# Latent attention in a two-layer encoder: probabilities scaled ahead of their turn, values at rest in the second product

## The chip, the core and the metric

The kernel runs on one core of a Trainium2 chip. The time is the device time of one execution in microseconds; before the change it is 1680.26 us, the median of three runs (1680.10 to 1680.61). The core has five engines with their own instruction queues: PE (TensorE, with PEld for its weight loads), DVE (VectorE), ACT (ScalarE), POOL (GpSimd) and SP (SyncE, which here issues the weight transfers). They meet by semaphores alone. TensorE writes its products into PSUM, which has eight banks; ACT and DVE read them out from there.

## What is computed

A trunk of two layers over 256 tokens, width 1024. Each layer normalises, projects once into three token mixers and three gates, merges the mixers, and goes on with a feed-forward part (dense in the first layer, eight experts in the second). The change lies in the third mixer, the latent attention, with eight heads of 64 values:

```python
for i in range(S // Q_BLOCK):                     # two blocks of 128 queries
    q0, k_end = i * Q_BLOCK, (i + 1) * Q_BLOCK
    s = (...q_nope k_nope + q_pe k_pe...) * scale
    s = jnp.where(k_chunk[None, :] <= q_chunk[:, None], s, -1e30)
    pr = jax.nn.softmax(s, axis=-1).astype(v.dtype)
    outs.append(jnp.einsum('bhqk,bkhe->bqhe', pr, v[:, :k_end]))
...
branch = jnp.einsum('bsnc,ncd->bsnd', ys, w_branch[l])   # ys: the three mixers' outputs
merged = jnp.sum(gates * branch, axis=2)
```

The first 128 queries see 128 keys and the second 128 see 256, so a head has 3 x 128 columns of probabilities.

## The kernel before

**The attention loop.** The loop over `i` stands once for each engine (lines 1580, 1150 and 2357), and the engines walk it together. In iteration `i`, PE computes the scores of head `i` (`sM`, lines 1587 and 1588), two units of the gate projection (line 1427; a unit is three fp32r products of 512 columns), then turns the probabilities of head `i - 1` with three transposes (`pT`, line 1595), multiplies the turned probabilities of head `i - 2` with the values (`oM`, lines 1601 to 1603: the probabilities are the weights at rest, 128x128, and 64 columns of values stream), and does two more gate units. DVE masks and scales the scores of head `i` into `sm`, takes the row maxima (lines 2364 to 2373), makes the low part of a gate weight quarter (`g_low`, line 2375, printed as line 2136), and for head `i - 2` takes the reciprocal of the row sum `den` and multiplies it onto the product while reading it out into `y_mla` (lines 2384 and 2387). In iterations 1 and 2 it also scales the retention's output `y_ret` (1024 columns each time). ACT exponentiates in place with the row sums accumulated (lines 1153 and 1155), copies the turned probabilities of head `i - 1` from PSUM to `pT` (line 1158, printed as 987), and at `i == 3` it applies the sigmoid to two gate tiles (lines 1160 and 1161), for which it loads another table and loads the exponential's again afterwards. POOL makes the high parts of the gate weights.

**After the loop** PE turns the inputs of the second mixer (`kT`, 16 transposes, line 1577, copied to `tT` by ACT), multiplies the last head, ends a gate panel with units 46 and 47, and turns the retention's output (`yT0`, line 1626). ACT then has a sigmoid with its table load again (`gate(4)`, `gate(5)`), and the copies of `yT0`, for which the second half of the products at line 1663 waits.

**The turn of the attention's output.** `y_mla` holds tokens in partitions. The branch projection needs channels there, so in the middle of the second mixer, for `t == 0`, PE turns it with eight transposes (`branch_in(2)`, line 1767, printed as 1626) and ACT copies it to `yT[2]` in two pieces (line 1228). They stand between the products of line 1731 and gate units 64 and 65.

**What sets the order.** Everything is written out by hand. `layer_jobs` lists each PSUM tile in the order in which PE makes it, with the engine that frees it; `place_jobs` gives each the bank that has been idle longest, and `bank(job)` makes PE wait until the tile before it in that bank has been freed. `read_out` waits until a tile has been read out. The weights come through a ring of three slots, filled by SP in the order of `panels`.

Of the kernel before, what the change touches and what calls it, by code (L numbers as in the profile page):

```python
# [17 lines left out]
P = 128  # L18
# [124 lines left out]
def layer_jobs(l):  # L143
# [15 lines left out]
    for i in range(NH + 2):  # L159
        out += [(f"sM{i}", V)] * (i < NH) + [(f"pT{i - 1}", A)] * (0 < i <= NH)  # L160
        out += [(f"kT0{hp}", A) for hp in range(4)] * (i > NH)
        out += [(f"oM{i - 2}", V)] * (i > 1)
        out += [(f"gt{2 + i // 8 * 2 + t}", A) for t in range(T if i == 3 or i > NH else 0)]
    out += [("yT00", A), ("yT01", A)]
    for t in range(T):
        out += [(f"kT1{hp}", A) for hp in range(4)] * t
        out += [(f"M{t}{i}", V) for i in PAIRED] + [(f"br0{t}{t}", V)]
        out += [(f"B{t}{u}", A) for u in range(NH // 2)]
        out += [("gt8", A), ("gt9", A), ("br210", V)] if t else [("gt6", A), ("gt7", A)]
        out += [(f"I{t}{g}", A) for g in range(2)]  # L170
        for lv in range(LEVELS):
            out += [(f"T{t}{lv}{g}", V) for g in range(2)]
            for g in range(2):
                out += [(f"X{t}{lv}{g}", V)] * (lv < LEVELS - 1) + [(f"XT{t}{lv}{g}", V)]
        out += [(("br001", "br201")[t], V), (f"Z{t}", A)] + [(f"W{t}{c}", A) for c in range(2)]
        out += [("yT10", A), ("dU20", V), ("dU21", V)] if t else [("yT20", A), ("yT21", A)]
        out += [(f"U{t}", A)]
        if t == 0:
            out += [("S1", V), ("br010", V), ("dU10", V), ("dU11", V), ("br200", V), ("S2", V)]
        else:  # L180
            out += [("S3", V), ("dU30", V), ("dU31", V), ("br211", V)]
        out += [(f"Y{t}{e}", A) for e in range(2)]
# [127 lines left out]
class Signals:  # L310


    def __init__(self, nc):
# [69 lines left out]
        self.prob_ready = new("prob_ready")  # L383
        self.merged_done = new("merged_done")
# [38 lines left out]
def build(nc, x, positions, all_gains, w_in, rwkv_mu, rwkv_w0, rwkv_w2, rwkv_a0, rwkv_a2, rwkv_g2, rwkv_k_k,  # L423
# [5 lines left out]
    def sb(name, shape, dt=F32, where=None):  # L429
# [29 lines left out]
    y_mla = sb("y_mla", [P, T, W], where=hn_at + 4096)  # L459
# [59 lines left out]
    yT = {n: sb(f"yT{n}", [P, 4, SEQ], where=w) for n, w in ((0, scratch + 4096), (2, ec_at - 4096))}  # L519
    yT1_hi = sb("yT1_hi", [P, 4, SEQ], F32R, where=scratch)  # L520
    yT1_lo = sb("yT1_lo", [P, 4, SEQ], F32R, where=hn_at + 4096)
# [4 lines left out]
        (B + 24576, B + 28672, B + 32768, B + 36864, B + 40960, scratch + 8192, B + 53248, ec_at - 4096))]  # L526
# [218 lines left out]
    def _(sp):  # L745
# [21 lines left out]
        for n, (kind, l, j, _) in enumerate(PANELS):  # L767
# [33 lines left out]
            elif kind == "mla":  # L801
                sp.dma_start(slot[:, 0:1536].rearrange("p (c n) -> p c n", c=2), rows(mla_w_qb[l])).then_inc(sem, 16)
                sp.dma_start(slot[:, 1536:2560], mla_w_kvb[l]).then_inc(sem, 16)
            elif kind == "branch":
# [163 lines left out]
    def _(act):  # L968
# [23 lines left out]
        for l in range(DEPTH):  # L992
# [156 lines left out]
            gate(1)  # L1149
            for i in range(NH + 1):  # L1150
                if i < NH:
# [4 lines left out]
                                          bias=smax[:, i, 1:2], accum_out=den[:, i, 1:2]), s.prob_ready)  # L1156
                if i:
                    copy_out(f"pT{i - 1}.{l}", pT[:, (i - 1) % 2, :], 384)
# [39 lines left out]
            for t in range(T):  # L1198
                for hp in range(4):
                    copy_out(f"kT{t}{hp}.{l}", tT[:, hp, :])  # L1200
                if t == 0:
                    gate(4)
                    gate(5)
# [23 lines left out]
                for u in range(0 if t else 2):  # L1227
                    copy_out(f"yT2{u}.{l}", yT[2][:, 2 * u:2 * u + 2, :])
# [138 lines left out]
    def _(pe):  # L1367
# [70 lines left out]
        for l in range(DEPTH):  # L1438
# [141 lines left out]
            for i in range(NH + 2):  # L1580
# [8 lines left out]
                if i < NH:  # L1589
                    gate_units(16 + 4 * i, 18 + 4 * i)  # L1590
                if 0 < i <= NH:
                    pe.wait_ge(s.prob_ready, NH * l + i)
# [23 lines left out]
            def branch_in(n):  # L1616

                if n == 2:
                    read_out(pe, f"oM{NH - 1}.{l}")
                else:  # L1620
                    pe.wait_ge(s.ret_done, l + 1)
                for u in range(2):
                    b = bank(f"yT{n}{u}.{l}")
                    for i in range(2):
                        for t in range(T):
                            ins = TR(b[:, 256 * i + 128 * t:256 * i + 128 * t + 128],
                                     (y_ret, None, y_mla)[n][:, t, 2 * u + i:W:4], ident)
                    done(ins)

            def branch_slot(n):  # L1630

                slot = panel_of("branch", l, n)
                read_out(pe, f"yT{n}1.{l}" if n != 1 else f"yT10.{l}")
# [16 lines left out]
            for t in range(T):  # L1650
                if t == 0:
                    branch_in(0)
# [113 lines left out]
                else:  # L1766
                    branch_in(2)
# [362 lines left out]
    def _(dve):  # L2130
# [56 lines left out]
        for l in range(DEPTH):  # L2187
# [169 lines left out]
            for i in range(NH + 2):  # L2357
# [16 lines left out]
                if i <= NH:  # L2374
                    g_low(6 + i)
# [638 lines left out]
```

## Time and profile before

| | |
|---|---|
| median of three runs | 1680.26 us (1680.10 to 1680.61) |
| span of the profiled execution | 1678.8 us |
| PE busy | 1624.5 us, 97% |
| DVE busy | 642.3 us, 38% |
| ACT busy | 444.0 us, 26% |
| granted TensorE clock, mean | 0.997 |
| attention loop, layer 0 | 146.6 to 180.5 us |
| turn of the attention's output, layer 0 | 219 us |

The span runs from the first to the last instruction of one profiled execution; the page shows no other time of that execution, and the timed runs are 1.5 us longer (1680.26 - 1678.8). Times inside the program are counted from the span's start. A row of a timeline has its start, its duration and the idle time that came before it on its engine, with what ended it. Durations of neighbouring PE rows overlap, because products are pipelined: what one costs is read from start to start. The chain of waits goes by ends, so the same instruction stands there about 0.2 us later.

### The profile page before, as it was taken

What the parts mean: (1) busy time and instruction counts of PE and PEld (TensorE: products, weight loads), DVE (VectorE), ACT (ScalarE), POOL (GpSimd) and SP (SyncE); (2) the same over time, 40 slices, a digit from 0 to 9 for tenths busy, and PEclk for the clock granted to TensorE, in tenths of its full rate; (3) what the DMA queues carried; (4) which work ended last, traced back from release to release, by engine and by line L of the source; (5) the groups of instructions that cost most, each with busy time, mean ns of one, the idle gap of its engine ahead of it and who ended that gap; (6) DMA issues with size and microseconds to landing.
All of it is one profiled execution on the core that took longest, in us unless ns stands there. A gap on an engine that the chain in (4) does not pass through costs nothing.

```text
span 1678.8 us, 34618 instructions
## 1 busy us (share of the span) xinstructions
PE 1624.5 (97%) x15590; PEld 1016.0 (61%) x15590; DVE 642.3 (38%) x1037; ACT 444.0 (26%) x652; POOL 171.7 (10%) x172
## 2 busy tenths in 40 slices
PE   8999999999999999999999999989999799999996
PEld 7878777788888877877754436343362434634433
DVE  6668666655555669657532010000100001000012
ACT  5477423454344566423410000000000000000001
POOL 1264002200000075100400000000000000000010
PEclk9999999999999999999999999999999999999998
DMA  9645213555445743212799999999999999999996
GB/s 347 234 146 201 86 63 118 212 203 186 171 170 201 225 175 110 101 52 101 306 425 429 428 430 428 429 429 429 429 428 427 429 429 429 428 428 420 406 427 256
DMA packets 84250, 494.14 MB, mean 294 GB/s; under 512 B 5528, under 2 KB 14612, under 8 KB 60632
## 3 DMA queue, kind: packets, MB, share of 16 engines
q1 hardware_dynamic: 79360, 480.52, 71.0%
q0 software_dynamic: 2064, 7.67, 1.2%
q10 hardware_dynamic: 2680, 3.74, 0.7%
q8 instruction: 124, 2.03, 0.4%
q14 instruction: 22, 0.18, 0.0%
HBM read 484.78 MB, written 6.16 MB: 292 GB/s over the span
## 4 chain that ended last, share of the span: by engine, by line
PE 81%; DMA 10%; DVE 6%; ACT 2%; issue 1%; SPq 0%; DVEq 0%; ACTq 0%
PE bank L1427 30%; PE bank L2073 26%; PE bank L2092 11%; DMA slot<-moe_units_dram 9%; PE bank L1642 3%; PE bank L1613 2%; PE bank L1419 2%; PE bank L2035 1%; PE bank L2007 1%; DVE ring_lo L2136 1%; DVE tmp L2136 0%; DMA ring<-w_in_dram 0%; PE bank L1997 0%; DVE xterm L2136 0%; DVE xc L2489 0%
## 5 line engine op out<-in xcount | busy, mean ns | idle before, releaser
L2073 PE MATMUL bank<-slot,xg 128*32 128x512 f32 (+1 forms) x5120 | 489.3, 539 | 8.9 <-DMA slot<-moe_units_dram 8.2
L2073 PEld LDWEIGHTS bank<-slot,xg 128*32 128x32 f32 x5120 | 168.5, 110 | 314.4 <-issue 278.7
L2092 PE MATMUL bank<-slot,ehT 128*32 128x256 f32 x4480 | 250.6, 381 | 25.3 <-DMA slot<-moe_units_dram 24.4
L2092 PEld LDWEIGHTS bank<-slot,ehT 128*32 128x32 f32 x4480 | 143.0, 110 | 127.7 <-DMA slot<-moe_units_dram 33.4
L2136 DVE TENSOR_TENSOR ehm<-bank,esg 128x512 f32<-128x512 f32 (+3 forms) x32 | 23.7, 741 | 463.6 <-ACT esg L1329 463.6
L1329 ACT ACTIVATE esg<-bank 128x512 f32<-128x512 f32 (+3 forms) x32 | 20.4, 637 | 491.9 <-PE bank L2073 491.9
L1427 PE MATMUL bank<-i_hi,ix_hi 128*128 128x512 f32 (+2 forms) x288 | 108.4, 376 | 2.0 <-DVE ix_lo L2136 1.0
L1427 PE MATMUL bank<-i_hi,ix_lo 128*128 128x512 f32 (+2 forms) x288 | 107.9, 375 | 0.0
L1427 PE MATMUL bank<-ring_lo,ix_hi 128*128 128x512 f32 (+2 forms) x288 | 107.8, 374 | 0.0
L2136 DVE TENSOR_TENSOR ring_lo<-ring,i_hi 128x2048 fp32r<-128x2048 f32 (+2 forms) x36 | 80.4, 2240 | 61.5 <-ACT i_hi L1007 61.5
L2908 DVE COPY ehT<-bank 128x512 f32<-128x512 f32 (+3 forms) x32 | 23.7, 741 | 208.6 <-PE bank L2035 203.0
L2136 DVE TENSOR_TENSOR ring_lo<-ring,f_hi 128x2048 fp32r<-128x2048 f32 (+1 forms) x36 | 75.5, 2112 | 63.4 <-ACT f_hi L1256 63.4
L1427 PE MATMUL bank<-g_hi,gx_hi 128*128 128x512 f32 x192 | 84.7, 441 | 0.5 <-DVE ring_lo L2136 0.5
L957 POOL TENSOR_TENSOR place_f<-place_f,cst 128x4 f32<-128x4 f32 x1 | 0.2, 194 | 773.2 <-PE bank L2073 773.2
L1427 PE MATMUL bank<-g_hi,gx_lo 128*128 128x512 f32 x192 | 75.3, 392 | 0.0
L1427 PE MATMUL bank<-ring_lo,gx_hi 128*128 128x512 f32 x192 | 75.2, 392 | 0.0
L1427 PE MATMUL bank<-f_hi,fx_hi 128*128 128x512 f32 (+1 forms) x192 | 71.7, 374 | 0.0
L1427 PE MATMUL bank<-f_hi,fx_lo 128*128 128x512 f32 (+1 forms) x192 | 71.3, 372 | 0.0
L1427 PE MATMUL bank<-ring_lo,fx_hi 128*128 128x512 f32 (+1 forms) x192 | 71.3, 371 | 0.0
L1256 ACT ACTIVATE f_hi<-ring 128x2048 fp32r<-128x2048 f32 (+1 forms) x36 | 62.6, 1770 | 32.5 <-DMA ring<-ffn_w_down_dram 18.5
L1007 ACT ACTIVATE i_hi<-ring 128x2048 fp32r<-128x2048 f32 (+2 forms) x36 | 62.8, 1788 | 24.0 <-issue 11.6
L2136 DVE TENSOR_TENSOR ring_lo<-ring,g_hi 128x1024 fp32r<-128x1024 f32 x48 | 61.7, 1288 | 5.8 <-POOL g_hi L932 4.5
(490 smaller groups left out, 2238.4 us busy)
## 6 DMA issues: line engine op xcount, KB each, us to landing
slot<-moe_units_dram SPq DMA_DIRECT2D x166, 2048.0 KB, 29.5
ring<-w_in_dram SPq DMA_DIRECT2D x25, 2048.0 KB, 8.9
ring<-w_branch_dram SPq DMA_DIRECT2D x6, 2048.0 KB, 7.9
ring<-ffn_w_gate_dram SPq DMA_DIRECT2D x5, 2048.0 KB, 7.9
ring<-ffn_w_up_dram SPq DMA_DIRECT2D x5, 2048.0 KB, 7.8
ring<-ffn_w_down_dram SPq DMA_DIRECT2D x5, 2048.0 KB, 7.9
ring<-w_o_dram SPq DMA_DIRECT2D x2, 2048.0 KB, 8.8
ring<-w_o_dram SPq DMA_DIRECT2D x4, 1024.0 KB, 6.2
```

Of the source, the lines that this page charges most:

```text
L1007: own.step(A.activation(i_hi[:, (q + 1) % 4, 0:width], src, ACT.Copy), s.i_hi_ready)
L1256: own.step(A.activation(f_hi[:, q % 4, 0:width], src, ACT.Copy), s.f_hi_ready)
L1329: A.activation(by_group(esg[:, 0:width], r), gate_, ACT.Silu).then_inc(s.silu_ready, 1)
L1419: ins = M(b[:, 0:width], lhs[:, c, t * P:(t + 1) * P], w[:, c, c0:c0 + width], start=c == 0, stop=c == k - 1)
L1427: ins = M(dst, a[:, c, tok], v[:, cols], start=start and n == 0, stop=stop and n == 2, skip_group_check=True)
L1613: ins = M(b[ch, cols], left[ch, :], right[ch, :], start=True, stop=True)
L1642: ins = M(dst[:], yT[n][:, c, t * P:(t + 1) * P], slot[:, D * c + 512 * u:D * c + 512 * u + 512], start=c == 0, stop=c == 3, skip_group_ch ...
L2007: ins = M(psum[:, to:to + SEL], h[:, t, c * P:c * P + P], sel[:, t, :], start=t == 0, stop=t == T - 1)
L2073: ins = M(psum[GROUP * p:GROUP * p + GROUP, to:to + width], xg[:, x, o:o + GROUP], w[:, c, p, :], start=x == 0 and to % 512 == 0, stop=x = ...
L2092: ins = M(psum[GROUP * p:GROUP * p + GROUP, o:o + 256], ehT[:, x, GROUP * i:GROUP * i + GROUP], w[:, c, p, :], start=x == 0 and o % 512 == ...
L2136: return V.tensor_tensor(out_, a, b, op)
L2908: V.tensor_copy(ehT[:, 8 * r:8 * r + n, 0:tokens].rearrange("p c (g k) -> p g c k", k=GROUP), psum[:, TURN:TURN + n * tokens].rearrange("p ...
```

## The change

For each head DVE now waits in the same iteration for the exponentials, takes the reciprocal of `den`, and multiplies it onto the probabilities in `sm` (128 and 256 columns) before PE turns them; PE's transposes wait for this (`scaled_ready`) instead of for the exponential. The second product is made for two heads at once, in the iterations 3, 5 and 7 and after the loop's last turn (`oP0` to `oP3`), with the values as weights at rest (128x64) and the turned probabilities streaming (256 and 128 columns); one head of a pair writes the bank's partitions 0 to 63, the other 64 to 127. The result has its channels in partitions, ACT copies it into `yT[2]`, and `y_mla`, its eight transposes and two copies are gone. The branch weights of the attention are loaded with another order of rows, in pieces of 1024 columns. Three buffers change places.

```diff
     for i in range(NH + 2):
-        out += [(f"sM{i}", V)] * (i < NH) + [(f"pT{i - 1}", A)] * (0 < i <= NH)
+        out += [(f"sM{i}", V)] * (i < NH)
         out += [(f"kT0{hp}", A) for hp in range(4)] * (i > NH)
-        out += [(f"oM{i - 2}", V)] * (i > 1)
+        out += [(f"oP{(i - 3) // 2}", A)] * (i > 2 and i % 2)
+        out += [(f"pT{i - 1}", A)] * (0 < i <= NH)
...
-        out += [("yT10", A), ("dU20", V), ("dU21", V)] if t else [("yT20", A), ("yT21", A)]
+        out += [("yT10", A), ("dU20", V), ("dU21", V)] if t else []
...
+            elif kind == "branch" and j == 2:
+                sp.dma_start(slot.rearrange("p (c n) -> p c n", c=4), w_branch[l, j].rearrange("(c p) n -> p c n", p=P))\
+                    .then_inc(sem, 16)
...
+            def latent_out(k):
+
+                copy_out(f"oP{k}.{l}", yT[2][:, k, :], SEQ)
+
             for i in range(NH + 1):
...
+                if i > 2 and i % 2:
+                    latent_out((i - 3) // 2)
                 if i:
                     copy_out(f"pT{i - 1}.{l}", pT[:, (i - 1) % 2, :], 384)
...
                 if t == 0:
+                    latent_out(3)
                     gate(4)
...
-                for u in range(0 if t else 2):
-                    copy_out(f"yT2{u}.{l}", yT[2][:, 2 * u:2 * u + 2, :])
...
+                if i > 2 and i % 2:
+                    k = (i - 3) // 2
+                    read_out(pe, f"pT{2 * k + 1}.{l}")
+                    b = bank(f"oP{k}.{l}")
+                    for c in range(T):
+                        for e in range(2):
+                            ins = M(b[64 * e:64 * e + 64, P * c:SEQ], mv[:, c, 2 * k + e, :],
+                                    pT[:, e, SEQ * c:SEQ + P * c], start=c == 0, stop=c == 1, skip_group_check=True)
+                    done(ins)
                 if 0 < i <= NH:
-                    pe.wait_ge(s.prob_ready, NH * l + i)
+                    pe.wait_ge(s.scaled_ready, NH * l + i)
...
-                if i > 1:
-                    k = i - 2
-                    read_out(pe, f"pT{k}.{l}")
-                    b = bank(f"oM{k}.{l}")
-                    M(b[:, 0:64], pT[:, k % 2, 0:128], mv[:, 0, k, :], start=True, stop=True)
-                    M(b[:, 64:128], pT[:, k % 2, 128:256], mv[:, 0, k, :], start=True, stop=False)
-                    done(M(b[:, 64:128], pT[:, k % 2, 256:384], mv[:, 1, k, :], start=False, stop=True))
...
                 else:
-                    branch_in(2)
                     gate_units(64, 66)
...
-                if i > 1:
-                    j = i - 2
-                    dve.wait_ge(s.prob_ready, NH * l + j + 1)
-                    step(V.reciprocal(den[:, j, :], den[:, j, :]))
-                    b = product(dve, f"oM{j}.{l}")
+                if i < NH:
+                    dve.wait_ge(s.prob_ready, NH * l + i + 1)
+                    step(V.reciprocal(den[:, i, :], den[:, i, :]))
                     settle()
-                    free(tt(y_mla[:, :, 64 * j:64 * j + 64], b[:, 0:128].rearrange("p (t e) -> p t e", t=T),
-                            wide(den[:, j, :], HD), ALU.mult), f"oM{j}.{l}")
+                    for t, keys in enumerate((slice(0, P), slice(P, 384))):
+                        step(V.tensor_scalar(sm[:, i % 2, keys], sm[:, i % 2, keys], den[:, i, t:t + 1], None, ALU.mult),
+                             s.scaled_ready if t else None)
```

**PE at the end of the attention loop of layer 0.** Before, from the gate products of iteration 7 on (`sm` holds the probabilities, `mv` the values, `kk` and `pr` are inputs of the second mixer):

```order
L1427 MATMUL bank<-g_hi_138,gx_lo 128x512
L1595 MATMUL bank<-cst,sm 128x128 x3
L1601 MATMUL bank<-mv,pT 128x64
L1602 MATMUL bank<-mv,pT 128x64
L1603 MATMUL bank<-mv,pT 128x64
L1595 MATMUL bank<-cst,sm 128x128 x3
L1601 MATMUL bank<-mv,pT 128x64
L1602 MATMUL bank<-mv,pT 128x64
L1603 MATMUL bank<-mv,pT 128x64
L1577 MATMUL bank<-cst,kk 128x128
```

And the same place in the changed kernel:

```order
L1437 MATMUL bank<-g_hi_137,gx_lo 128x512
L1607 MATMUL bank<-pT,mv 64x256 x2
L1607 MATMUL bank<-pT,mv 64x128 x2
L1614 MATMUL bank<-cst,sm 128x128 x6
L1587 MATMUL bank<-cst,kk 128x128
```

The pair product `oP2` now stands ahead of the transposes, the turns of heads 6 and 7 follow each other with nothing between them, and the inputs of the second mixer are turned right behind the last head.

**ACT from the exponential of head 3 to that of head 4.** Before (`sm,den` is the exponential with its row sum, `sig` the sigmoid of the gates):

```order
L1153 ACTIVATE sm,den<-sm,smax 128x128
L1155 ACTIVATE sm,den<-sm,smax 128x256
L987 ACTIVATE pT<-bank 128x384
L1142 ACT_TABLE_LOAD
L1142 ACTIVATE sig_113<-bank,stat 128x512 x2
L1153 ACT_TABLE_LOAD
L1153 ACTIVATE sm,den<-sm,smax 128x128
L1155 ACTIVATE sm,den<-sm,smax 128x256
L987 ACTIVATE pT<-bank 128x384
```

In the changed kernel:

```order
L1162 ACTIVATE sm,den<-sm,smax 128x128
L1164 ACTIVATE sm,den<-sm,smax 128x256
L991 ACTIVATE yT_116<-bank 128x256
L991 ACTIVATE pT<-bank 128x384
L1146 ACT_TABLE_LOAD
L1146 ACTIVATE sig_112<-bank,stat 128x512 x2
L1162 ACT_TABLE_LOAD
L1162 ACTIVATE sm,den<-sm,smax 128x128
L1164 ACTIVATE sm,den<-sm,smax 128x256
L991 ACTIVATE pT<-bank 128x384
```

The copy of the pair product comes in front of the copy of the turned probabilities; the two table loads and the sigmoids stay where they were, ahead of the exponential of head 4.

## Rows read from the trace of the kernel before

**Rows 1.** the page, section 2 (DMA, 40 slices) and section 4 (chain by engine)

```profile
DMA  9645213555445743212799999999999999999996
...
PE 81%; DMA 10%; DVE 6%; ACT 2%; issue 1%; SPq 0%; DVEq 0%; ACTq 0%
```

**Rows 2.** timeline of PE in the attention of layer 0: start us, us, instruction

```profile
152.02 0.49 PE L1595 MATMUL bank<-cst,sm 128*128 128x128 f32 x3
152.26 0.48 PE L1427 MATMUL bank<-g_hi,gx_hi 128*128 128x512 f32 x1
...
169.07 0.49 PE L1595 MATMUL bank<-cst,sm 128*128 128x128 f32 x3
...
169.99 0.48 PE L1427 MATMUL bank<-g_hi,gx_hi 128*128 128x512 f32 x1
...
175.90 0.39 PE L1587 MATMUL bank<-mkT,mqT 96*128 96x128 f32 x2
...
179.37 0.55 PE L1595 MATMUL bank<-cst,sm 128*128 128x128 f32 x3 [0.32 <-ACT sm L1155]
...
180.46 0.28 PE L1577 MATMUL bank<-cst,kk 128*128 128x128 f32 x1
...
182.21 0.33 PE L1601 MATMUL bank<-mv,pT 128*128 128x64 f32 x2
```

**Rows 3.** chain of waits, 219 to 225 us: start us, us, what

```profile
219.31 1.16 PE bank L1626 x8
220.47 1.40 PE bank L1427 x6
221.87 1.08 PE bank L1613 x32
222.95 1.58 PE bank L1427 x6
```

**Rows 4.** chain of waits, 183 us: the sigmoid table load after the attention

```profile
183.18 1.28 ACT L1142
```

**Rows 5.** timeline of ACT, 160 to 167 us and at 219 us

```profile
160.65 0.40 ACT L1153 ACTIVATE sm<-sm,smax 128x128 f32<-128x128 f32 x1 [2.81 <-DVE smax L2373]
...
162.03 1.28 ACT L1142 ACT_TABLE_LOAD   x1
...
165.90 0.40 ACT L1153 ACTIVATE sm<-sm,smax 128x128 f32<-128x128 f32 x1
...
166.80 0.47 ACT L987 ACTIVATE pT<-bank 128x384 f32<-128x384 f32 x1
...
219.09 0.66 ACT L987 ACTIVATE nw<-bank 128x256 f32<-128x256 f32 x2
```

**Rows 6.** timeline of DVE, 150 to 159 us: heads 1 to 3

```profile
150.83 0.29 DVE L2364 SCALAR_TENSOR_TENSOR sm<-bank,cst 128x128 f32<-128x128 f32 x1 [0.73 <-PE bank L1588]
...
154.91 0.29 DVE L2364 SCALAR_TENSOR_TENSOR sm<-bank,cst 128x128 f32<-128x128 f32 x1
...
157.48 1.22 DVE L2136 TENSOR_TENSOR y_ret<-y_ret,raw 128x1024 f32<-128x1024 f32 x1
158.62 0.15 DVE L2384 RECIPROCAL den<-den 128x2 f32<-128x2 f32 x1
158.88 0.29 DVE L2136 TENSOR_TENSOR y_mla<-bank,den 128x128 f32<-128x128 f32 x1
159.09 0.28 DVE L2364 SCALAR_TENSOR_TENSOR sm<-bank,cst 128x128 f32<-128x128 f32 x1
```

**Rows 7.** instructions of line 2291: duration ns min/median/max

```profile
L2291 DVE TENSOR_SCALAR qa<-qa,stat x4: 348/352/353, 109.2 to 621.5; 128x256 f32<-128x256 f32 x4
```

**Rows 8.** timelines of PE at 224 us and of PEld at 870 us

```profile
224.62 0.29 PE L1758 MATMUL bank<-pr 64*64 64x64 f32 x4
224.74 0.33 PE L1757 MATMUL bank<-uu,ab 64*64 64x64 f32 x4
...
870.41 0.16 PEld L2073 LDWEIGHTS bank<-slot,xg 128*32 128x32 f32 x4 [0.27 <-issue]
```

More of the change, by code:

```diff
@@ L383, in __init__ @@
         self.prob_ready = new("prob_ready")
+        self.scaled_ready = new("scaled_ready")
         self.merged_done = new("merged_done")
@@ L458, in build @@
     y_ret = sb("y_ret", [P, T, W], where=hn_at)
-    y_mla = sb("y_mla", [P, T, W], where=hn_at + 4096)
     ring_at = at[0]
@@ L517, in build @@
     assert VEC_AT["lnx"][0] * 4 >= 16384
-    yT = {n: sb(f"yT{n}", [P, 4, SEQ], where=w) for n, w in ((0, scratch + 4096), (2, ec_at - 4096))}
+    yT = {n: sb(f"yT{n}", [P, 4, SEQ], where=w) for n, w in ((0, scratch + 4096), (2, hn_at + 4096))}
     yT1_hi = sb("yT1_hi", [P, 4, SEQ], F32R, where=scratch)
-    yT1_lo = sb("yT1_lo", [P, 4, SEQ], F32R, where=hn_at + 4096)
+    yT1_lo = sb("yT1_lo", [P, 4, SEQ], F32R, where=ec_at - 4096)
     gT_hi = sb("gT_hi", [P, KD, SEQ], F32R, where=B + 16384)
@@ L525, in build @@
     k_hi = [sb(f"k_hi{n}", [P, QUARTER], F32R, where=w) for n, w in enumerate(
-        (B + 24576, B + 28672, B + 32768, B + 36864, B + 40960, scratch + 8192, B + 53248, ec_at - 4096))]
+        (B + 24576, B + 28672, B + 32768, B + 36864, B + 40960, scratch + 8192, B + 53248, hn_at + 4096))]
     k_hi_last = {n: sb(f"k_hi_last{n}", [P, QUARTER], F32R, where=w) for n, w in ((5, B + 45056), (7, B + 49152))}
@@ L1614, in by_chunk, with turn_retention @@
                 return ins
[L1616 to L1621, printed above, removed]
+            def turn_retention():
+                pe.wait_ge(s.ret_done, l + 1)
                 for u in range(2):
-                    b = bank(f"yT{n}{u}.{l}")
+                    b = bank(f"yT0{u}.{l}")
                     for i in range(2):
                         for t in range(T):
-                            ins = TR(b[:, 256 * i + 128 * t:256 * i + 128 * t + 128],
-                                     (y_ret, None, y_mla)[n][:, t, 2 * u + i:W:4], ident)
+                            ins = TR(b[:, 256 * i + 128 * t:256 * i + 128 * t + 128], y_ret[:, t, 2 * u + i:W:4], ident)
                     done(ins)
@@ L1632, in branch_slot @@
                 slot = panel_of("branch", l, n)
-                read_out(pe, f"yT{n}1.{l}" if n != 1 else f"yT10.{l}")
+                read_out(pe, ("yT01", "yT10", "oP3")[n] + f".{l}")
                 return slot
@@ L1651, in _ @@
                 if t == 0:
-                    branch_in(0)
+                    turn_retention()
                 else:
@@ L2355, in _ @@
             g_low(5)
-            for i in range(NH + 2):
+            for i in range(NH + 1):
                 if i < NH:
@@ L2373, in _ @@
                     step(V.tensor_scalar(smax[:, i, :], smax[:, i, :], -1.0, None, ALU.mult), s.masked_ready)
-                if i <= NH:
-                    g_low(6 + i)
+                g_low(6 + i)
                 if i == 1:
```

## The prediction, made before the changed kernel was run

> **What bounds the kernel now.** I read the page first: TensorE is busy in 97% of the span, and the chain of work that ended last runs through PE for 81% of it, through the DMA for 10% [rows 1]. The DMA share stands in the last half, where every slice reads 9. That is the expert stage, behind the second layer: it starts when the second layer ends and is bound by its own weight stream, so a microsecond that a layer gives up comes out at the end unchanged. The attention and the second mixer stand once in each layer, and layer 1 repeats layer 0; each gain below counts twice. The second view was the timeline of PE in the attention. PE stands still there only once, for 0.32 us ahead of the last head's turn [rows 2] (start 179.37): from the exponential of head 7 on, the heads' chain through PE, DVE and ACT decides, not PE's work. Third, the timelines of ACT and DVE over the same heads: both have gaps in a steady iteration (ACT 2.81 us ahead of head 3's exponential) [rows 5, 6], but two stretches have none. DVE runs on without a pause from head 2 to head 3, because the retention's multiplies stand there [rows 6], and ACT has one block from the exponential of head 3 to that of head 4, 165.90 - 160.65 = 5.25 us with two sigmoids between two table loads [rows 5]. Behind the attention the chain goes over ACT: its table load starts at 183.18 [rows 4]. In the second mixer it runs over PE without a gap at the eight transposes [rows 3].
>
> **What goes.** One head's product `oM` costs PE (169.99 - 169.07) - (152.26 - 152.02) = 0.92 - 0.24 = 0.68 us: the first distance, from a turn to the next gate product, has it, the second hasn't [rows 2]. Eight go. The transposes of `y_mla` go too: with them the gate units start 1.16 us later and take 1.40; without them the units follow the 64x64 products directly, as they do further down, where they take 1.58. So 1.16 + 1.40 - 1.58 = 0.98 us per layer [rows 3]. This is the path, and what is late next there is still PE: the 64x64 products follow the gates immediately. ACT's two copies of `yT[2]` lay beside PE and give nothing.
>
> **What comes: the pair product.** Each of two heads needs 256 + 128 = 384 streamed fp32 columns, in its own 64 columns of the array. The trace doesn't have such a product. The nearest row is the 64x64 work of the second mixer: four instructions, two products in each of two quarters of the array, follow the next four after 224.74 - 224.62 = 0.12 us [rows 8]. At 0.115 us for 64 columns in both, 384 columns cost 6 x 0.115 = 0.69 us if the two heads run side by side, and 1.38 if they run one after the other. That column tiles do run side by side with all 128 rows in use, I take from the expert stage: four weight loads of 128x32 every 0.16 + 0.27 = 0.43 us, a group for four tiles [rows 8]. A gate product behind the tiles is 1.58 - 1.40 = 0.18 us late [rows 3], and the 32 small products take 1.08 where 8 x 0.115 = 0.92 is their work, 0.16 to get in [rows 3, 8]. So X, the cost of a pair product, is 0.69 + 0.18 + 0.16 = 1.03 us; I take 1.04. The bounds are 0.69 (the two switches cost nothing, for the halves stand in one column split and keep all rows) and 1.38 + 0.35 = 1.73.
>
> The Trainium skill bears on both parts. "TensorEngine Tiling (Array Packing)", Key Properties, says that a change of the tiling mode drains the engine; the 0.18 us of [rows 3] agree. "TensorE: Matmul & The Clock Gate", Part 3 (The mechanism), says that products start and end strictly in program order. As the fp32 product is two passes, both of one head stand ahead of the first of the other, so that only neighbours overlap: 0.23 + 0.23 + 0.23 + 0.115 + 0.115 = 0.92 instead of 0.69, by passes of half of [rows 8]'s price. The mechanism in this kernel's terms is a partly staggered pair, X = 1.27, and the sum below comes to 1679.3 with it. Rows 8 speak against it, since there too two instructions in a row belong to one tile.
>
> **What comes: the scaling.** DVE now waits for the exponentials of the same head, takes the reciprocal (0.26 us to the next start) and multiplies 128 columns (0.21, the distance from the 128 wide multiply to the next instruction) [rows 6], and 256 columns, which take 0.352 to their end [rows 7] and some 0.27 to the next start. So 0.73 us for DVE each head, and 0.26 + 0.20 + 0.35 = 0.81 us between the exponential and the turn; with one more hop between engines (0.06, my estimate; 0.11 lie between the end of the reciprocal and the multiply in [rows 6]) 0.87. In a steady iteration this is hidden by the four gate units: the turn of head `i` comes an iteration behind its scores. Queued behind DVE's new wait is the mask of the next head. It is not hidden in two places.
>
> First, heads 1 to 3. Head 1 starts on DVE at 150.83 as before. Head 2 comes at 154.91 + 0.73 = 155.64; head 3 2.57 + 1.14 + 0.73 later [rows 6] (157.48 - 154.91, 158.62 - 157.48), at 160.08 instead of 159.09. Its exponential follows 1.56 us behind (160.65 - 159.09), at 161.64. ACT's full block of 5.25 us, longer by the copy of `oP0` (256 columns: 0.33 each where they are read [rows 5]; I take 0.36), puts the exponential of head 4 at 167.25. The copy of head 3's turned probabilities comes 0.90 later and takes 0.47 [rows 5]: it ends at 168.62. PE needs it for `oP1`, which stands where the turn of head 4 stood at 169.07; three `oM` are gone ahead of it and one pair product has come: 169.07 - 2.04 + 1.04 = 168.07. PE waits 0.55 us, a wait that isn't there now.
>
> Second, the end. From `oP1` to the scores of head 7 PE has 1.04 + (175.90 - 169.07) - 2 x 0.68 = 6.51 us, so `sM7` starts at 175.13 (before: 175.90). Its turn follows 3.47 us later today (179.37 - 175.90) [rows 2], and 0.87 more now: 179.47. PE needed 179.37 - 0.32 - 175.90 = 3.15 from the scores to this wait, and needs 3.15 - 0.68 + 1.04 = 3.51 now: it is there at 178.64 and waits 0.83. From the turn of head 7 to the second mixer's inputs it was 1.09 with `oM6`, now 0.41; the 16 transposes take 182.21 - 180.46 = 1.75 [rows 2]; `oP3` starts at 181.63, ends 1.04 later, shows its result 0.21 behind the next start (0.33 - 0.12 in [rows 8]) and is copied in 0.36: 183.24. Then comes the sigmoid's table load, which stood at 183.18 [rows 4]. The attention loses 0.06 us.
>
> **The sum.** 0.98 - 0.06 = 0.92 us per layer, 1.84 in all, against the profiled span of 1678.8: 1677.0. The timed runs are 1.46 us longer than that span, so 1680.26 - 1.84 = 1678.4. Each 0.1 us on X counts 0.2 us per layer (once for `oP1`, once for `oP3`; `oP0` is swallowed by the wait, `oP2` too). X = 0.69 gives 0.92 + 0.70 = 1.62 per layer and 1677.0. The branch weights come in longer pieces of fewer rows; ring slot and need are some 20 us apart there, so I cost this at nothing; the copies onto `yT[2]` stand on ACT ahead of another copy and cost only what is counted. What I call no change is a move within 0.2% (3.36 us), about what a measurement of this kernel can tell from none.
>
> **The rivals.**
> A, the forecast: 1678.4, its own range 1677.0 to 1679.3 by X from 0.69 to 1.27. Chance 0.67.
> B, PE's work alone decides: the scaling is hidden everywhere, since PE reaches its waits later than I think or DVE sooner. Then a layer gains 8 x 0.68 + 0.98 - 4 x 1.04 = 2.26 us: 1675.7. With only the wait ahead of `oP1` gone (0.55) it is 1677.3. For it: PE is 81% of the chain. Against it: the head 7 chain has no slack today, it already holds PE for 0.32 us [rows 2]. Chance 0.14.
> C, slower: the halves of the array run one after the other, X = 1.73. PE is then at `oP1` at 168.76 without a wait, `sM7` starts at 168.76 + 1.73 + 5.47 = 175.96, its turn at 180.30, `oP3`'s copy ends at 184.76: 1.58 lost, 0.98 gained, 0.60 lost per layer: 1681.5. It decides from X = 1.50 on. For it: four instructions in a row for two tiles, as in no row with full 128 rows and 64 columns. Against it: both rows of [rows 8]. Chance 0.11.
> D, the missing transposes pay nothing, because DVE's or ACT's part of the second mixer is as late as PE: 1680.4. For it: the mixer runs over three engines. Against it: PE stands alone in the chain there, without a gap [rows 3]. Chance 0.08.
>
> Below 1676.9 lie B and a tail of A, 0.17; above 1683.6 only C with something on top, 0.03; the rest, 0.80, is no measurable change. The range takes in most of B and of C's distance: 1676.0 to 1681.0.
>
> **What the changed kernel's profile would show.** Right, if PE waits some 0.5 us for ACT's copy of the turned probabilities ahead of `oP1`, and about 0.8 us for DVE's scaling ahead of the turn of head 7; if a pair product takes 1.0 us from its start to the turn behind it; if the scores of head 7 start near 175.1 and the table load near 183.2; and if the gate units in the second mixer follow the 64x64 products 0.98 us sooner against their neighbours. Wrong, if pair products take 1.7 us (C) or 0.7; if PE never waits for the scaling (B); if a wait for DVE or ACT of about 1 us has come into the second mixer where the transposes were (D); or if a DMA wait appears ahead of the attention's branch product.

## The result: 0.18% slower, where 0.11% faster was forecast

| | before | changed |
|---|---|---|
| median (15 runs each) | 1680.30 us (1679.88 to 1681.48) | 1683.56 us (1682.85 to 1684.26) |
| ratio, 95% interval | | 1.0018 (1.0011 to 1.0025) |
| span of the profiled execution | 1678.8 us | 1681.7 us |
| DVE busy, POOL busy | 642.3, 171.7 us | 653.8, 172.2 us |

The forecast was 1678.4 with a range of 1676.0 to 1681.0: the time lies 5.2 us above the one and 2.6 us above the other. The page of the changed kernel, sections 2 and 4, answers to [rows 1]:

```profile
DMA  9745223555545743212799999999999999999996
...
PE 78%; DMA 9%; DVE 9%; ACT 2%; issue 1%; SPq 0%; DVEq 0%; ACTq 0%
```

The expert stage is bound by its DMA as before, but DVE has gone from 6% to 9% of the chain. Where this is, the timeline of PE in the attention of layer 0 shows. The columns are those of [rows 2]; the last bracket is the wait and what ended it:

```profile
157.66 0.55 PE L1614 MATMUL bank<-cst,sm 128*128 128x128 f32 x3 [1.10 <-DVE sm L2392]
...
162.86 0.55 PE L1614 MATMUL bank<-cst,sm 128*128 128x128 f32 x3 [0.43 <-DVE sm L2392]
...
171.23 0.87 PE L1607 MATMUL bank<-pT,mv 128*64 128x256 f32 x8 [0.59 <-ACT pT L991]
172.03 0.55 PE L1614 MATMUL bank<-cst,sm 128*128 128x128 f32 x3
...
177.56 0.38 PE L1597 MATMUL bank<-mkT,mqT 96*128 96x128 f32 x2
...
182.52 0.55 PE L1614 MATMUL bank<-cst,sm 128*128 128x128 f32 x3 [1.49 <-DVE sm L2392]
```

Before, PE waited once, for 0.32 us. Now it waits four times: 1.10 us for DVE's scaling of head 1, 0.43 for head 2, 0.59 for ACT's copy ahead of `oP1`, and 1.49 for head 7. Two of the four were forecast, at 0.55 and 0.83. The timeline of ACT answers to [rows 4, 5]:

```profile
164.28 0.40 ACT L1162 ACTIVATE sm<-sm,smax 128x128 f32<-128x128 f32 x1 [3.84 <-DVE smax L2380]
...
169.81 0.40 ACT L1162 ACTIVATE sm<-sm,smax 128x128 f32<-128x128 f32 x1
...
186.07 1.28 ACT L1146 ACT_TABLE_LOAD   x1
```

To compare executions whose first weight load took different time (8.13 us before, 8.72 in this one), I count from the first scores `sM0`, which start at 146.58 before and at 147.19 now. The table load behind the attention stood at 183.18 - 146.58 = 36.60 and stands at 186.07 - 147.19 = 38.88: the attention loses 2.28 us where 0.06 was forecast. In layer 1 it is 36.61 and 38.87.

What caused it stands in DVE's timeline, beside GpSimd's. DVE:

```profile
150.84 1.43 DVE L2392 TENSOR_SCALAR sm<-sm,den 128x128 f32<-128x128 f32 x2
...
154.99 1.83 DVE L2143 TENSOR_TENSOR y_ret<-y_ret,stat 128x1024 f32<-128x1024 f32 x1
...
157.05 0.55 DVE L2392 TENSOR_SCALAR sm<-sm,den 128x128 f32<-128x128 f32 x2
...
160.09 2.06 DVE L2143 TENSOR_TENSOR y_ret<-y_ret,raw 128x1024 f32<-128x1024 f32 x1
...
162.72 0.28 DVE L2371 SCALAR_TENSOR_TENSOR sm<-bank,cst 128x128 f32<-128x128 f32 x1
...
165.50 1.11 DVE L2392 TENSOR_SCALAR sm<-sm,den 128x128 f32<-128x128 f32 x2
...
174.28 1.14 DVE L2392 TENSOR_SCALAR sm<-sm,den 128x128 f32<-128x128 f32 x2
...
178.11 1.11 DVE L2392 TENSOR_SCALAR sm<-sm,den 128x128 f32<-128x128 f32 x2
```

GpSimd (POOL), the casts that make the high parts of the gate weights:

```profile
150.89 1.04 POOL L936 CAST g_hi<-ring 128x1024 fp32r<-128x1024 f32 x1 [3.87 <-PE bank L1437]
154.58 1.16 POOL L936 CAST g_hi<-ring 128x1024 fp32r<-128x1024 f32 x1 [2.65 <-PE bank L1437]
159.66 1.41 POOL L936 CAST g_hi<-ring 128x1024 fp32r<-128x1024 f32 x1 [3.92 <-PE bank L1437]
164.87 1.41 POOL L936 CAST g_hi<-ring 128x1024 fp32r<-128x1024 f32 x1 [3.79 <-PE bank L1437]
...
174.03 1.04 POOL L936 CAST g_hi<-ring 128x1024 fp32r<-128x1024 f32 x1 [3.95 <-PE bank L1437]
177.79 1.09 POOL L936 CAST g_hi<-ring 128x1024 fp32r<-128x1024 f32 x1 [2.72 <-PE bank L1437]
```

One scaling pair (`x2`) takes 0.55 us when it is alone (157.05) and 1.11 to 1.43 when a cast runs: the pair of 150.84 ends at 152.27, 0.34 behind the cast that ends at 151.93; that of 165.50 at 166.61, 0.33 behind the cast's 166.28. The 0.33 is about the length of the second multiplication (256 columns, 0.34). It is the first, of 128 columns, that is stretched: 1.17 and 0.86 instead of 0.29, to 0.08 behind the cast's end both times. It hasn't run slowly beside the cast, it has stood until the cast was over. The `y_ret` multiplies that begin inside a cast take 1.83 and 2.06 instead of 1.22. And a cast that begins inside a DVE instruction is the one that stands: 159.66 and 164.87 take 1.41 instead of 1.04. Not every instruction in SBUF is stretched: the reciprocal ahead of the pair of 165.50 (165.30) lies inside the cast too and takes its usual 0.17. In the kernel before, `y_ret` came first and the cast lost, off everybody's path. DVE and GpSimd there:

```profile
153.65 1.22 DVE L2136 TENSOR_TENSOR y_ret<-y_ret,stat 128x1024 f32<-128x1024 f32 x1
```

```profile
153.97 1.81 POOL L932 CAST g_hi<-ring 128x1024 fp32r<-128x1024 f32 x1 [2.65 <-PE bank L1427]
```

The second mixer did what was forecast. The chain there answers to [rows 3]:

```profile
221.62 1.59 PE bank L1437 x6
223.21 1.08 PE bank L1625 x32
224.29 1.58 PE bank L1437 x6
```

The units that followed the transposes in 1.40 us now follow the 64x64 products in 1.59, and the 1.16 of the transposes are gone: 1.16 + 1.40 - 1.59 = 0.97 us. No wait for DVE, ACT or a DMA has come in there or ahead of the attention's branch product.

From layer to end: at the expert stage's first gather (861.30 against 858.68) the changed kernel is 2.62 us late. 0.61 of this is the later first scores, which don't belong to the change: the kernel before with another edit (E2 below) has them at 147.43. So 2.01 us are left, where the two layers should lose 2 x (2.28 - 0.97) = 2.62. In layer 0 the mixer's product at 220.86 is only 1.70 later counted from `sM0`, not 2.28, because the execution before lost time there (32 small products take 1.58 us at 214.83, with 0.17 of idle time, and 1.15 in layer 1). Against E2 the product is 2.22 later and the gather 2.87. One pair of executions thus carries this sum to within some 0.9 us only; the timed runs say 1.8 to 4.2 us (0.11% to 0.25%), and 2.62 lies inside.

### The profile page after: what moved, and what is told of

It reads as the page before. It is cut to its first block, busy times and chain, and to the rows that moved or that the text cites. A ratio compares the mean times of both kernels' runs of the same rounds, so it can differ in the third digit from the quotient of the medians.

```text
span 1681.7 us, 34518 instructions
## 1 busy us (share of the span) xinstructions
PE 1619.0 (96%) x15542; PEld 1006.3 (60%) x15542; DVE 653.8 (39%) x1053; ACT 444.2 (26%) x656; POOL 172.2 (10%) x172
## 4 chain that ended last, share of the span: by engine, by line
PE 78%; DMA 9%; DVE 9%; ACT 2%; issue 1%; SPq 0%; DVEq 0%; ACTq 0%
PE bank L1437 27%; PE bank L2080 26%; PE bank L2099 11%; DMA slot<-moe_units_dram 9%; PE bank L1650 3%; DVE ring_lo L2143 2%; PE bank L1429 2%; PE bank L1625 2%; PE bank L2042 1%; PE bank L2014 1%; DMA ring<-w_in_dram 1%; DVE tmp L2143 0%; DVE sm L2392 0%; PE bank L2004 0%; DVE xterm L2143 0%
```

## The experiments

Each ratio is to runs of the kernel before on the same chip, with its 95% interval.

**E1, the casts cut short.** In the loop GpSimd casts 16 columns instead of 1024 for quarters 6 and 8 to 15; the high parts of those weights are left out.

```diff
+                if n > 5 and n != 7:
+                    G.tensor_copy(g_hi[G_PLACE[n]][:, 0:16], g_quarter(l, n)[:, 0:16]).then_inc(s.pool_g_hi_ready, 1)
+                    continue
                 G.tensor_copy(g_hi[G_PLACE[n]][:], g_quarter(l, n)).then_inc(s.pool_g_hi_ready, 1)
```

> The changed kernel, but GpSimd's casts of gate weight quarters 6 and 8 to 15 copy 16 of 1024 columns (the high parts of those weights are left out), so that GpSimd is all but idle in the attention loop. Theory P (port): in the changed kernel DVE's scaling of a head takes 1.1 to 1.4 us instead of 0.55 whenever a cast runs beside it (150.84, 165.50, 174.28, 178.11), and the two multiplies of y_ret take 1.83 and 2.06 instead of 1.22. Without the casts every scaling pair takes 0.55, the y_ret multiplies 1.22, PE's wait ahead of the turn of head 1 (1.10) and head 7 (1.49) shrink to under 0.3 and about 0.9, and the table load behind the attention, 2.3 us late in each layer now, comes about 2 us sooner: some 1679.7. Rival O (order): the loss comes from DVE waiting for the exponentials of its own head, whatever GpSimd does: the long pairs stay or the waits do, 1683.5.

Measured: 1677.49 us (1676.43 to 1679.21), ratio 0.9979 (0.9970 to 0.9988). Lower than expected. The scaling instructions of both layers in the changed kernel and here (duration ns min/median/max):

```profile
L2392 DVE TENSOR_SCALAR sm<-sm,den x32: 285/344/1168, 150.8 to 694.8; 128x128 f32<-128x128 f32 x16, 128x256 f32<-128x256 f32 x16
```

```profile
L2395 DVE TENSOR_SCALAR sm<-sm,den x32: 285/334/350, 150.8 to 688.7; 128x128 f32<-128x128 f32 x16, 128x256 f32<-128x256 f32 x16
```

The longest falls from 1168 to 350 ns, the `y_ret` multiplies are 1.22 again, PE waits 0.27 and 0.78 us in place of four waits, and the table load comes at 36.01. Rival O is out: the order is the same, and only the casts are gone.

**E2, the control.** The same edit in the kernel before, with the same parts left out.

> Control: the kernel before with the same short casts (the same high parts are left out). Its timeline shows no DVE instruction of the loop stretched beside a cast, so theory P and rival O both expect no change: 1680.3, within 0.5 us, which also tells that the short casts by themselves free nothing on PE.

Measured: 1679.87 us (1679.15 to 1680.46), ratio 0.9994 (0.9985 to 1.0003). The table load stays at 36.61. The 1.1 us between the medians isn't told from no change. Without the change there is no collision on the path to remove; E1's gain belongs to the change.

**E3, the retention's multiplies later.**

```diff
-                if i == 1:
-                    group_scale(y_ret[:], 0, P, 3 * l)
-                if i == 2:
+                if i == 4:
                     dve.wait_ge(s.silu_g_ready, l + 1)
                     step(tt(y_ret[:], y_ret[:], raw[:, 3, :, :], ALU.mult), s.ret_done)
...
                              s.scaled_ready if t else None)
+                if i == 3:
+                    group_scale(y_ret[:], 0, P, 3 * l)
```

> The changed kernel with the two multiplies of y_ret moved from iterations 1 and 2 to the end of iteration 3 and ahead of the wait for the exponential in iteration 4, where DVE sits idle 1.65 us behind ACT's two table loads. Theory H (heads 1 to 3 are late because y_ret's 3.9 us stand on DVE ahead of their scaling): PE waits neither for head 1's turn (1.10) nor head 2's (0.43), ACT's exponential of head 4 comes some 2 us sooner, the table load behind the attention about 1.7 us sooner in each layer: near 1680.3. Rival E (the end decides: the DVE loop of heads 4 to 7 is full with its stretched scalings, 3.8 us a head, and the wait for head 7 sits there anyway): the early gain is lost again at head 7, at least 1683.

Measured: 1682.57 us (1680.90 to 1690.67), ratio 1.0014 (1.0004 to 1.0023). Neither theory was right in full. The early waits are gone and the scores of head 7 come 28.96 us behind the first ones instead of 30.37, but other pairs met casts (1.43, 1.11, 1.11, 1.11, 1.11), the moved multiplies met casts in their new places too (1.88 and 2.06), PE waits 0.97 us for head 4 and 1.81 for head 7, and the table load comes at 37.78. In layer 1 it comes at 39.45, for a reason of its own. The last turn there, and the view of 693.5 to 696.3 us (PE, PEld, DVE, ACT and POOL busy, then the granted clock, DMA share and GB/s):

```profile
692.82 0.75 PE L1614 MATMUL bank<-cst,sm 128*128 128x128 f32 x3 [1.81 <-DVE sm L2390]
```

```profile
693.50:696.30 2.80, 2.80 (x15) 2.80 (x14) 0.41 (x1) 1.81 (x4) 0.00 (x0) 0.50 0.00 0
```

Behind the wait of 1.81 us the granted clock is 0.50, the lower level of 1.2 GHz, and the 16 transposes take 0.21 us each instead of 0.11. In layer 0 the same wait had no such fall (1.00 from 182.0 to 184.8 us). What decides between the two stays open.

**E4, no scaling.** The two multiplications are left out; the reciprocal frees the turn.

```diff
-                    step(V.reciprocal(den[:, i, :], den[:, i, :]))
-                    settle()
-                    for t, keys in enumerate((slice(0, P), slice(P, 384))):
-                        step(V.tensor_scalar(sm[:, i % 2, keys], sm[:, i % 2, keys], den[:, i, t:t + 1], None, ALU.mult),
-                             s.scaled_ready if t else None)
+                    step(V.reciprocal(den[:, i, :], den[:, i, :]), s.scaled_ready)
```

> The changed kernel without the two multiplications of the probabilities by 1/den (left out); the reciprocal stays and frees the turn. What the layout alone is worth. Both P and H expect that only the y_ret multiplies still meet a cast; DVE has 1.44 + 1.13 + 0.20 us a head and is no bound, head 7's turn comes 0.5 us or more sooner than with an undisturbed scaling: 1677.5. If the layout itself (the pair product, 0.8 us each in place of 2 x 0.68) costs more than it shows, the time stays above 1680.

Measured: 2096.05 us, ratio 1.247, which says nothing on the attention. Other numbers send tokens to more experts: 7680 expert products here against 5120 in the changed kernel.

```profile
L2080 PE MATMUL bank<-slot,xg 128*32 128x512 f32 (+1 forms) x5120 | 489.7, 539 | 11.1 <-DMA slot<-moe_units_dram 8.0
```

```profile
L2080 PE MATMUL bank<-slot,xg 128*32 128x512 f32 (+1 forms) x7680 | 736.9, 541 | 24.2 <-DMA slot<-moe_units_dram 21.6
```

I should have foreseen that a part left out ahead of a router changes the work behind it. The trace up to the expert stage can be read: the table load comes at 35.08 and the expert stage's first gather 706.52 us behind `sM0`, against 712.10 before. The layout alone would be worth 5.6 us over two layers by this pair of executions, and 2 x (36.60 - 35.08 + 0.97) = 5.0 by the stages.

**E5, the casts held back.** The whole computation; a cast waits until DVE has scaled the head.

```diff
+                if 6 < n < 15:
+                    pool.wait_ge(s.scaled_ready, NH * l + n - 6)
                 G.tensor_copy(g_hi[G_PLACE[n]][:], g_quarter(l, n)).then_inc(s.pool_g_hi_ready, 1)
```

> The changed kernel complete, but GpSimd's cast of quarter 7 + i waits until DVE has scaled head i, so that it runs beside the next head's mask (which reads PSUM) instead of beside the scaling or the y_ret multiplies. Theory P (the port): no scaling pair over 0.6 us, the y_ret multiplies 1.22, the table load behind the attention 36.0 to 36.1 us behind the first scores as with the short casts (38.88 in the changed kernel, 36.60 before). The short casts gave 1677.49, of which 1.1 us came without the change too (the control), so this should be 1678.5, under the kernel before by some 1.8. Rival W (the work of the casts, not their place): the casts now come too late for the low parts, DVE waits for GpSimd and PE for DVE, and the time stays at 1683 or above.

Measured: 1677.82 us (1677.08 to 1679.16), ratio 0.9983 (0.9974 to 0.9992). DVE, GpSimd, PE and ACT in layer 0:

```profile
150.39 0.55 DVE L2394 TENSOR_SCALAR sm<-sm,den 128x128 f32<-128x128 f32 x2
...
153.81 1.22 DVE L2145 TENSOR_TENSOR y_ret<-y_ret,stat 128x1024 f32<-128x1024 f32 x1
...
156.45 0.29 DVE L2379 TENSOR_REDUCE smax<-sm 128x1 f32<-128x128 f32 x1
156.65 0.41 DVE L2380 TENSOR_REDUCE smax<-sm 128x1 f32<-128x256 f32 x1
...
158.31 1.22 DVE L2145 TENSOR_TENSOR y_ret<-y_ret,raw 128x1024 f32<-128x1024 f32 x1
...
160.10 0.28 DVE L2373 SCALAR_TENSOR_TENSOR sm<-bank,cst 128x128 f32<-128x128 f32 x1
```

```profile
151.07 1.04 POOL L938 CAST g_hi<-ring 128x1024 fp32r<-128x1024 f32 x1 [6.46 <-DVE sm L2394]
155.98 1.04 POOL L938 CAST g_hi<-ring 128x1024 fp32r<-128x1024 f32 x1 [3.86 <-DVE sm L2394]
```

```profile
168.59 0.87 PE L1609 MATMUL bank<-pT,mv 128*64 128x256 f32 x8 [0.26 <-ACT pT L993]
...
174.94 0.38 PE L1599 MATMUL bank<-mkT,mqT 96*128 96x128 f32 x2
...
179.20 0.55 PE L1616 MATMUL bank<-cst,sm 128*128 128x128 f32 x3 [0.78 <-DVE sm L2394]
```

```profile
167.18 0.40 ACT L1164 ACTIVATE sm<-sm,smax 128x128 f32<-128x128 f32 x1
...
182.74 1.28 ACT L1148 ACT_TABLE_LOAD   x1
```

The work of the casts is all there, at its full 1.04 us each, and nothing of DVE's in the loop is stretched: they run beside the mask of the next head, which reads PSUM, and beside its row maxima. These read `sm` in SBUF and still take 0.29 and 0.41 us inside the cast of 155.98, as they do alone. The table load comes at 182.74 - 146.75 = 35.99. Theory P holds and W is out. With 1.04 us moved by a wait on another semaphore, the change turns from 0.18% slower into 0.17% faster.

**E6, casts held and the retention's multiplies later** (the edits of E3 and E5 together).

> The same, with the two y_ret multiplies moved to iterations 3 and 4 as well. If they cost what they do only by meeting a cast, moving them is worth at most the 0.27 us that PE still waits ahead of the second pair product: 1678.0 to 1678.9, no difference from casts held alone. If heads 1 to 3 are late through the multiplies' own length, 1677 or less.

Measured: 1677.28 us (1676.23 to 1678.40), ratio 0.9980 (0.9971 to 0.9989), not told apart from E5. The wait ahead of `oP1` is gone, the table load comes at 35.66: 0.33 us a layer, a little over the 0.27 expected at most. The time lies between the two expectations (from 1678.0 and up to 1677) and decides neither. One of the moved multiplies still meets a held cast:

```profile
162.04 2.10 DVE L2145 TENSOR_TENSOR y_ret<-y_ret,stat 128x1024 f32<-128x1024 f32 x1
```

It costs nothing on the path, since behind it DVE has to wait for ACT's full block anyway. What matters is not whether two instructions collide, but where.

**E7, the pair product head by head** (with the casts held).

```diff
-                    for c in range(T):
-                        for e in range(2):
+                    for e in range(2):
+                        for c in range(T):
```

> Casts held, and the pair product issued head by head: both products of the one head, then both of the other, instead of in turn. From its start to the next start a pair product takes 0.80 us in the changed kernel. If the two heads run beside each other because the next instruction of the other half may pass one of this half, order is nothing and it stays 0.80. If products start in program order, only the second pass of the last product of one head and the first of the other overlap: 1.1 to 1.3 us, and the kernel is some 0.8 us longer in all.

Measured: 1677.36 us (1676.99 to 1677.82), ratio 0.9980 (0.9970 to 0.9990). PE:

```profile
159.90 0.88 PE L1609 MATMUL bank<-pT,mv 128*64 128x256 f32 x8
160.71 0.55 PE L1616 MATMUL bank<-cst,sm 128*128 128x128 f32 x3
```

0.81 us from start to start: the order makes no difference, and the two halves run beside each other. Taken one by one, the second head's 256 columns start 0.01 us behind the first head's, and 0.47 ahead of the first head's 128 columns, which stand in front of them in the program.

**E8, ACT scales heads 4 to 7** (casts as in the changed kernel).

```diff
+                if 3 < i < NH:
+                    act.wait_ge(s.recip_ready, 4 * l + i - 3)
+                    own.step(A.activation(sm[:, i % 2, 0:128], sm[:, i % 2, 0:128], ACT.Copy,
+                                          scale=den[:, i, 0:1]))
+                    own.step(A.activation(sm[:, i % 2, 128:384], sm[:, i % 2, 128:384], ACT.Copy,
+                                          scale=den[:, i, 1:2]), s.scaled_ready)
...
-                    step(V.reciprocal(den[:, i, :], den[:, i, :]))
+                    step(V.reciprocal(den[:, i, :], den[:, i, :]), s.recip_ready if i > 3 else None)
                     settle()
-                    for t, keys in enumerate((slice(0, P), slice(P, 384))):
+                    for t, keys in enumerate((slice(0, P), slice(P, 384)) if i < 4 else ()):
```

> The changed kernel, with ACT instead of DVE multiplying heads 4 to 7 by 1/den (behind its copy of the head before; DVE takes the reciprocals), the casts where they were. Theory P: the stretched pairs of heads 5 and 6 are gone, those of heads 0 and 3 and the stretched y_ret multiplies stay, so the exponential of head 4 is as late as it was (22.6 us behind the first scores), but from there PE waits only for head 7: half of the loss or less comes back, 1681.5 to 1682.5. Rival A (ACT becomes the bound, its 0.9 us of exponentials, 0.5 of copy and 0.9 of scaling in one chain): 1683.5 or more.

Measured: 1684.13 us (1682.93 to 1685.47), ratio 1.0022 (1.0013 to 1.0031). My expectation fell, the number is rival A's. PE:

```profile
170.91 0.87 PE L1614 MATMUL bank<-pT,mv 128*64 128x256 f32 x8 [0.58 <-ACT pT L992]
...
182.48 0.55 PE L1621 MATMUL bank<-cst,sm 128*128 128x128 f32 x3 [1.75 <-ACT sm L1178]
```

The scores of head 7 come at 30.29 as in the changed kernel (30.37), so taking the stretched pairs of heads 5 and 6 away gave nothing up to there. The turn of head 7 waits 1.75 us now: ACT's scaling stands behind two copies, 181.64 to 182.43 for an exponential that began at 180.11, 2.37 us in all where DVE took 1.82 (180.70 to 182.52).

**E9, only the first three casts held** (`6 < n < 10`).

> The changed kernel with only the first three casts of the loop (quarters 7 to 9) held back until heads 0 to 2 are scaled; the later ones start as before. It parts the loss into its two places. If the stretched instructions of heads 0 to 2 make ACT's block with its table loads late, and those of heads 3, 5 and 6 only fill DVE ahead of head 7, the scores of head 7 come 28.2 us behind the first ones, as with all casts held (30.37 in the changed kernel), head 7's turn is up to 0.7 us later behind them than the 4.26 us there, and the table load lies between 36.0 and 36.7: 1678 to 1679.3. Rival (every stretched instruction counts alike): three of six stretches are left, the scores of head 7 come near 29.3 and the kernel takes about 1681.

Measured: 1680.85 us (1679.85 to 1683.01), ratio 1.0002 (0.9993 to 1.0011). The time is the rival's; the scores of head 7 come at 28.94, between the two expectations, and the table load at 37.43. PE waits 0.22 us for head 3, 0.58 ahead of `oP1` and 1.48 for head 7. The first wait of 1.10 us and the second are gone, but the edit made a collision of its own. GpSimd and DVE:

```profile
160.72 2.03 POOL L938 CAST g_hi<-ring 128x1024 fp32r<-128x1024 f32 x2 [3.29 <-DVE sm L2394]
```

```profile
161.87 0.91 DVE L2382 TENSOR_SCALAR smax<-smax 128x2 f32<-128x2 f32 x1
```

The held cast and the free one behind it ran back to back until 162.75, and the small negation of the row maxima, two columns from SBUF to SBUF, took 0.91 us instead of 0.17. The exponential of head 3 and ACT's full block behind it were late by that. So E9 doesn't part the loss cleanly, and how much each of its two places costs stays open. It shows that an instruction of two columns can be held up as well; the reciprocals of `den`, of two columns too, were not (0.17 at most, 6 of the 16 beside a cast).

## Why the prediction was wrong

Counted from `sM0`, the steps as forecast, in the changed kernel, and with the casts held (E5):

| step | forecast | changed | casts held |
|---|---|---|---|
| DVE starts head 3 | 13.50 | 15.53 | 13.35 |
| exponential of head 4 | 20.67 | 22.62 | 20.43 |
| `oP1` starts | 22.04 | 24.04 | 21.84 |
| scores of head 7 | 28.55 | 30.37 | 28.19 |
| turn of head 7 | 32.89 | 35.33 | 32.45 |
| table load | 36.66 | 38.88 | 35.99 |
| pair product, start to the turn behind | 1.0 | 0.80 | 0.80 |

**The failed step** is "0.73 for DVE each head", together with the "2.57 + 1.14" of the `y_ret` multiplies in the same working: both were costed from rows in which no instruction of DVE's was held up, and the change moves DVE's instructions against the casts. From the reciprocal to the next mask DVE takes 0.66 us in E5, under the 0.73, but 1.55 and 1.24 beside a cast (150.64 to 152.19, 165.30 to 166.54); from one mask to the next, head 2 to head 3, it takes 5.20 us where 4.44 were forecast. The prediction read PE, DVE and ACT and left GpSimd's timeline out. E1, E2 and E5 show the cause: with the casts short or held the third column comes out within 0.7 us of the forecast everywhere. Without the change the short casts are worth nothing on this path.

How a loss of 0.06 us became 2.28: the first pair was 0.88 too long (1.43), the `y_ret` multiplies 0.61 and 0.84. Together 2.33, and head 3 starts 2.18 us later than with the casts held. The full block on ACT (5.25 us before, 5.53 now) passes that on to the exponential of head 4 (2.19) and to the scores of head 7 (2.18). The turn of head 7 is 2.88 late, 0.70 more, since with two stretched pairs DVE has no free time between heads (its mask of head 7 starts at 179.15, 1.59 behind the scores at 177.56, against 0.86 in E5). That DVE was full between heads 2 and 3 and that ACT's block would carry a delay through was right in the prediction; it had the right places and too short instructions. What a heavier DVE does to POOL and POOL to DVE was in none of the rivals.

Two things look better than they are. The wait ahead of `oP1` was forecast at 0.55 and is 0.59, by luck: PE and ACT were both 2 us late there, and undisturbed it is 0.26 (E5). And the move of 3.3 us lies within the 0.2% (3.36 us) that the prediction called no change, but the interval of the ratio tells it from none.

**The pair product.** From its start to the turn behind it, it took 0.80 us, where the prediction looked for 1.0. Its X of 1.04 also held the way into the tiled stretch. Counted so, X is 0.95 us: in E5 the last gate product ahead of `oP0` and the first behind the turn start at 159.48 and 160.90, 1.42 apart, and 155.72 and 156.19, 0.47 apart, where a turn alone lies between. The prediction's 0.69 + 0.18 + 0.16 had the ways in and out at 0.34 us together; with the same 0.69 they are some 0.26. The staggered pair (1.27) and the halves one after the other (1.73) are out, by E7 too. The Trainium skill's "TensorE: Matmul & The Clock Gate", Part 3 (The mechanism), with starts and ends in program order, would have made E7 longer; the trace doesn't show that. Of the 0.67 us between 36.66 and 35.99 at the table load, the pair products explain 0.45: from `oP1` to the scores of head 7 PE takes 6.35 us for 6.51, from `oP3` to the table load it is 1.32 for 1.61. The rest is small differences, not traced.

**The transposes.** 0.98 forecast, 0.97 measured. Rival D is out.

**The sum.** A layer was to gain 0.92; with the casts held it gains 36.60 - 35.99 + 0.97 = 1.58. In both layers that is 3.2 us; the medians show 2.8 (0.9983 of 1680.6). Rival B (1675.7) would have needed PE never to wait, which no run with the scaling showed.

The runs show the collision and its price; what the two engines share, no run here can show. The Trainium skill names it. "SBUF — State Buffer", SBUF: two separate sides, says that DVE and GpSimd share one pair of ports, held as an exclusive lock for a whole instruction, by a DVE instruction in a mode of two ports or with two SBUF inputs. The trace agrees with how long the loser waits (to the end of the other's instruction) and, but for one case, with who waits (whoever came second): the pair of 150.84 began 0.05 us ahead of the cast and stood all the same. It agrees with which of DVE's instructions are concerned: the scaling, the negation and the `y_ret` multiplies, which have two inputs in SBUF, were held up; masks that read PSUM, row maxima and reciprocals were not. That the scaling ran in a mode of two ports is seen only indirectly: 128 columns more cost it 0.06 us (0.29 and 0.35), and the row maximum 0.12 (0.29 and 0.41).

## What to carry to other kernels

A new instruction on DVE that reads and writes SBUF is costed beside GpSimd's timeline, not only beside DVE's own: here it cost its duration plus what was left of the cast it met, less 0.14 to 0.22 us. An added instruction also moves the old ones against the casts: the larger part of this loss, 1.45 of 2.33 us, fell on the `y_ret` multiplies, which the change doesn't touch. Where both are periodic, tie the GpSimd instruction to a semaphore behind the DVE work that is on the path, so that it falls beside PSUM reads and reductions; here this moved the kernel from 1.0018 to 0.9983 with two lines. And an engine with a full block (ACT's two table loads) passes every delay ahead of it on undiminished.

## What the runs showed of the hardware

- One DVE multiplication of 128 columns took 0.29 us alone and up to 1.17 beside a cast of GpSimd; a negation of two columns 0.17 and 0.91. Row maxima (0.29 and 0.41) and reciprocals (0.17) took the same beside a cast and alone. A cast of 1.04 us that came second took 1.41, and 1.81 in the kernel before.
- Two fp32 products in two column halves of the array, with all 128 rows, run beside each other in whatever order they are issued: 0.80 and 0.81 us for 2 x 384 columns. Issued half by half, the second half's first product starts 0.47 us ahead of the first half's second one.
- After a wait of PE of 1.81 us the granted clock was 0.50 over the next 2.8 us read in one layer and 1.00 in the other, in one execution.
